# Encoder trunk on one core: the attention stage one unit of weights later, one join of transposed heads moved, and no turn of x in the last layer

## The reference

```
h  = RMSNorm(x);  z = h @ W_in          # 6656 columns: A q,k,v | B q,k,v | pool | gates
A  = attention of 8 query heads on 2 key heads (QK-norm, axial rotary)
B  = dilated window attention, 3 groups of 4 heads (QK-norm, rotary), combined per slot
C  = multi-scale mean pooling minus the token, per-group linear map, scale
x += (sig(g0)*(A@Wa) + sig(g1)*(B@Wb) + sig(g2)*(C@Wc)) @ W_out
x += (silu(h2@W_gate) * (h2@W_up)) @ W_down ,  h2 = RMSNorm(x)
```

## Time and profile before

| | |
|---|---|
| median of 3 runs | 816.54 us (815.59 to 817.21) |
| the profiled execution | 815.6 us, of which the span from first to last instruction is 813.8 us |
| granted PE clock in the span | 1.000 of full speed |
| PE, DVE, ACT, POOL busy | 804.8, 570.9, 464.6, 234.9 us |
| read from HBM | 149.91 MB |

### The profile page before, as it was taken

The page is one execution under the profiler, slowest core; times in us unless marked ns, Lnnn a source line. Parts: engine busy times, 40 slices in busy tenths (PEclk is TensorE's granted clock), DMA queues, the critical chain, the costliest instruction groups (busy, mean ns, idle before and its releaser), DMA issues.

```text
span 813.8 us, 9827 instructions
## 1 busy us (share of the span) xinstructions
PE 804.8 (99%) x3816; PEld 661.1 (81%) x3816; DVE 570.9 (70%) x688; ACT 464.6 (57%) x535; POOL 234.9 (29%) x206
## 2 busy tenths in 40 slices
PE   8999999999999999999999999999999999999998
PEld 7877787888888888888888877878888888888886
DVE  5899865857776676665379997676696666676552
ACT  5778876583454455543457888765735454455430
POOL 1443324130033444430023242414100444444200
PEclk9999999999999999999999999999999999999999
DMA  9787787765457767685456887677554667876660
GB/s 336 284 237 209 217 219 208 220 195 193 155 200 213 228 214 203 219 246 212 164 202 198 222 219 221 206 221 204 179 199 165 220 206 211 226 232 213 195 214 38
DMA packets 98318, 170.22 MB, mean 209 GB/s; under 512 B 78016, under 2 KB 78176, under 8 KB 80864
## 3 DMA queue, kind: packets, MB, share of 16 engines
q1 hardware_dynamic: 96352, 163.34, 65.1%
q0 software_dynamic: 1632, 6.18, 2.6%
q10 hardware_dynamic: 288, 0.08, 0.0%
HBM read 149.91 MB, written 1.05 MB: 186 GB/s over the span
## 4 chain that ended last, share of the span: by engine, by line
PE 87%; DMA 4%; ACT 4%; DVE 3%; issue 2%; SPq 1%; DVEq 0%
PE bank L1124 27%; PE bank L1126 27%; PE bank L1135 27%; DMA w_raw<-in_stream_dram 4%; PE bank L1244 2%; PE bank L1157 1%; ACT w_hi L654 1%; PE bank L1212 1%; PE bank L1221 1%; PE bank L1184 1%; ACT qkT L732 1%; DVE zqk L937 0%; PE bank L1190 0%; DVE scratch L933 0%; ACT head_halves L726 0%
## 5 line engine op out<-in xcount | busy, mean ns | idle before, releaser
L843 DVE TENSOR_TENSOR w_lo<-w_raw,w_hi 128x2048 fp32r<-128x2048 f32 x134 | 316.7, 2365 | 116.7 <-ACT w_hi L654 116.4
L654 ACT ACTIVATE w_hi<-w_raw 128x2048 fp32r<-128x2048 f32 x134 | 256.5, 1915 | 169.8 <-DMA w_raw<-in_stream_dram 169.7
L1124 PE MATMUL bank<-w_hi,aT_hi 128*128 128x512 f32 x832 | 327.9, 394 | 2.0 <-ACT zvu L810 2.0
L1126 PE MATMUL bank<-w_hi,aT_lo 128*128 128x512 f32 x832 | 324.3, 390 | 0.0
L1135 PE MATMUL bank<-w_lo,aT_hi 128*128 128x512 f32 x832 | 223.3, 390 | 0.2 <-DVE w_lo L843 0.2
L1124 PEld LDWEIGHTS bank<-w_hi,aT_hi 128*128 128x128 f32 x832 | 156.2, 188 | 38.9 <-ACT zvu L810 2.9
L1135 PEld LDWEIGHTS bank<-w_lo,aT_hi 128*128 128x128 f32 x832 | 155.6, 188 | 32.9 <-DVE w_lo L843 0.7
L1126 PEld LDWEIGHTS bank<-w_hi,aT_lo 128*128 128x128 f32 x832 | 156.3, 188 | 31.7
L593 POOL COPY halves<-hid 128x512 uint16<-128x512 uint16 x44 | 75.7, 1748 | 4.6 <-DVE hid L1096 4.6
L602 POOL COPY hT_raw<-turned 128x512 uint16<-128x512 uint16 x44 | 33.8, 813 | 133.3 <-DMA turned<-halves 133.3
L1124 PE MATMUL bank<-w_hi,hT_hi 128*128 128x512 f32 x176 | 68.7, 390 | 0.0
(11 more groups left out here) (101 smaller groups left out, 794.3 us busy)
## 6 DMA issues: line engine op xcount, KB each, us to landing
w_raw<-in_stream_dram SPq DMA_DIRECT2D x135, 1024.0 KB, 5.2
bias_sb<-in_b_gate_dram POOLq DMA_DIRECT2D x12, 256.0 KB, 3.7
par<-in_params_dram POOLq DMA_DIRECT2D x3, 384.0 KB, 3.6
w_raw<-in_stream_dram SPq DMA_DIRECT2D x4, 256.0 KB, 5.1
pool_mat<-in_pooling_dram POOLq DMA_DIRECT2D x1, 1024.0 KB, 5.9
out_dram<-x_sb SPq DMA_DIRECT2D x4, 256.0 KB, 4.0
x_sb<-in_x_dram SPq DMA_DIRECT2D x2, 256.0 KB, 4.6
x_sb<-in_x_dram SPq DMA_DIRECT2D x1, 512.0 KB, 7.3
```

The source lines that it names most:

```text
L654: nc.scalar.activation(w_hi[:, j % RING, :, :].rearrange("p k n -> p (k n)"), w_raw[:, j % RING, :, :].rearrange("p k n -> p (k n)"), ACT. ...
L843: nc.vector.tensor_tensor(w[0], w[1], w[2].bitcast(F32), ALU.subtract).then_inc(unit_lo, 1)
L1124: nc.tensor.matmul(o, src[0][:, k, tok], w_hi[:, slot, wk + i, :], start=first and i == 0, stop=False)
L1126: nc.tensor.matmul(o, src[1][:, k, tok], w_hi[:, slot, wk + i, :], start=False, stop=False)
```

## The change

The softmax chain starts at unit 10 instead of 9, so that scores stand in units 10, 14, 18 and 22, exponentials in even units and the cutting of probabilities in odd ones. The attention outputs and the pooled products are moved by one unit with it; the pool turns stay. Of the A queries only token tile 0 is joined in unit 7; tile 1 is joined in unit 10 behind the exponentials, and the second group of scores waits for it. In the last layer the two turns of x for a next layer (8 transposes on PE, two scalings and two subtractions on DVE, two copies on ACT) are left out. In unit 61 of the first layer ACT does one exponential of a 128x2 tile, which brings the table of exponentials in there. The copying out of z became a function of its own, called in the same order (`FIRST_OUT` = (99, 0) never applies).

```
-JOINS_BEHIND = {7: [(0, 0), (0, 1)], 14: [(2, 0)], ...
+JOINS_BEHIND = {7: [(0, 0)], 10: [(0, 1)], 14: [(2, 0)], ...
-PAIR_UNIT = 9
+PAIR_UNIT = 10
+FIRST_OUT = (99, 0)
+EXP_TABLE_UNIT = 61
 TURNS_WITHIN = {
-    14: [("pool", 0)], 16: [("pool", 1), ("o", 0)], 19: [("o", 1)], 20: [("mixed", 0)], 22: [("mixed", 1)],
-    23: [("o", 2)], 27: [("o", 3)], 30: [("merged", 0), ("merged", 1)],
+    14: [("pool", 0)], 16: [("pool", 1)], 17: [("o", 0)], 20: [("o", 1)], 21: [("mixed", 0)], 23: [("mixed", 1)],
+    24: [("o", 2)], 28: [("o", 3)], 30: [("merged", 0), ("merged", 1)],
-def turns_before(t):
+def turns_before(t, lay=0):
     out = list(TURNS_BEFORE.get(t, []))
+    if lay == DEPTH - 1:
+        out = [name for name in out if name[0] != "mix_x"]
...
+                    if lay + 1 < DEPTH and t == EXP_TABLE_UNIT:
+                        nc.scalar.activation(table_warm[:, :], neg_half[:, 0, 0:MT], ACT.Exp)
...
+                if p == 2:
+                    wait_joined(pe, lay, (0, 1))
```

More of the change, by code:

```diff
@@ L84 @@
 JOINS_AHEAD = {8: [(1, 0), (1, 1)], 13: [(3, 0)]}
-JOINS_BEHIND = {7: [(0, 0), (0, 1)], 14: [(2, 0)], 15: [(4, 0)], 16: [(4, 1), (5, 0)], 17: [(3, 1)],
+JOINS_BEHIND = {7: [(0, 0)], 10: [(0, 1)], 14: [(2, 0)], 15: [(4, 0)], 16: [(4, 1), (5, 0)], 17: [(3, 1)],
                 18: [(2, 1), (5, 1)]}
@@ L732, in join_heads, with take_z @@
                 nc.scalar.activation(joined_heads(r, m), turned_heads(r, m), ACT.Copy).then_inc(heads_joined, 1)
+            def take_z(lay, c, m):
+                if c == 0 and m == 0:
+                    act.wait_ge(x_norm, lay * 2 + 1)
+                if c == 4 and m == 0:
+                    act.wait_ge(mask_ready, 1)
+                wait_full(act, lay, (f"z{c}", m))
+                for off, w, to, at in Z_PIECES[c]:
+                    dst = (zqk if to == "qk" else zvu)[:, m, at:at + w]
+                    src = B((f"z{c}", m))[:, off:off + w]
+                    if c == 0:
+                        dst = dst.rearrange("p (j g d) -> p g j d", g=2, d=HD)
+                        src = src.rearrange("p (g j d) -> p g j d", g=2, d=HD)
+                    if to == "qk":
+                        square = squares[:, m, at:at + w]
+                        if c == 0:
+                            square = square.rearrange("p (j g d) -> p g j d", g=2, d=HD)
+                        nc.scalar.activation(square, src, ACT.Square, scale=rstd[:, 0, m:m + 1])
+                    last = nc.scalar.activation(dst, src, ACT.Copy, scale=rstd[:, 0, m:m + 1])
+                free(last, (f"z{c}", m))
             def x_squares(lay, m, half):
@@ L746, in _ @@
                 for t in range(UNITS):
-                    for name in turns_before(t):
+                    for name in turns_before(t, lay):
                         turn(lay, name)
@@ L765, in _ @@
                         split_probs(lay, 2 * p + 1)
+                    if t == FIRST_OUT[0]:
+                        take_z(lay, t // 2, FIRST_OUT[1])
                     p = pair_at(t, 0)
@@ L791, in _ @@
                     if t % 2 == 1 and t // 2 <= POOL_CHUNK:
[L792 to L796, removed]
-                        for m in range(MT):
[L798 to L807, removed]
-                                        square = square.rearrange("p (j g d) -> p g j d", g=2, d=HD)
-                                    nc.scalar.activation(square, src, ACT.Square, scale=rstd[:, 0, m:m + 1])
-                                last = nc.scalar.activation(dst, src, ACT.Copy,
-                                                            scale=rstd[:, 0, m:m + 1])
-                            free(last, (f"z{c}", m))
+                        for m in range(MT):
+                            if (t, m) != FIRST_OUT:
+                                take_z(lay, t // 2, m)
                     if t in (U_OUT + 3, U_FFN):
@@ L1035, in _ @@
                         dve.wait_ge(gains_loaded, lay * 16 + 16)
-                    turns(lay, turns_before(t))
+                    turns(lay, turns_before(t, lay))
                     if t == 0:
```

## The result

The kernel after takes 810.46 us (median of 6 runs, 810.13 to 810.82), the kernel before 817.05 us (6 runs, 815.59 to 817.51). The ratio is 0.9921, with the 95% interval [0.9909, 0.9934]. The profiled execution of after took 810.14 us, with a span of 808.3; that of before 815.6 and 813.8.

What follows compares the result with a forecast made beforehand. PE, busy 804.8 of 813.8 us, bounds the kernel. 1.6 + 2.3 + 0.8 = 4.7, 4.8 with slower first matmuls, less 0.4 is 4.4: 815.6 becomes 811.2, median 812.1; range for 8 in 10, 810.8 to 814.6.

Steps and rivals of the forecast that it cites:

- Scores out of unit 9: Start of unit 9: moving the scores removes their wait for ACT's join, 1.2 us in layer 0, 0.4 in layer 1.
- the wait for z5: Before unit 12, both layers: PE's wait for the bank ACT copies into `zvu` goes, 2.3 us with twice the overlap.
- x: End of the last layer: 8 transposes on PE go, 0.8 us, with nothing waited for on either side.
- I put 0.4 us for both layers: Allowance for new waits at three thinly covered z banks, units 12 to 16; bounds nothing and about 3 us.
- The first cover: Bank 0 before unit 12, layer 0: free at 78.15, PE wants it at 78.25, so 0.1 us of cover.
- The second: z6's bank after unit 13's weights go out late: free at 90.8, wanted at 91.15, so 0.35 us of cover.
- step (b): z7, unit 15: POOL's late join delays unit 17's weights five us; bank free 105.3, wanted 105.5, cover 0.2 us.
- The median of the runs is 0.9 above it, so 812.1: Whole kernel: adds 0.9 us to the profiled execution's expected 811.2 to get the median of the runs.
- Rival A: Waits return at z's banks; if both `zvu` waits keep their size, gain 2.5 us, time 814.0; chance 0.15.
- B: Unit 17's weights: both join copies run behind a `w_lo`, unit 16 waits 3.5 us each layer, 818.7; chance 0.05.
- C: Unit 28: the last output comes late and holds up B's product, 0.5 us a layer, 813.1; chance 0.05.
- D: Scores wait in unit 10 as in unit 9, for something else on ACT; only x's 0.8 us stay, 815.7; chance 0.05.

Runs made afterwards that it cites:

- after_u19: Kernel after with two additions (128 x 512 each) on VectorE in unit 19 of both layers, ahead of z9's gates; 811.03 us, ratio 0.9939 to before.
- join_stays: Kernel after with q tile 1 of A joined in unit 7 again; 811.45 us, ratio 0.9944 to before.
- no_table: Kernel after without the exponential in unit 61, so the table loads in unit 10 of layer 1 again; 810.95 us, ratio 0.9938 to before.
- before_late: Kernel before with two more copies of 128 x 1024 on ACT in unit 1 of layer 0; 816.89 us against 815.63, ratio 1.0009.
- before_u19: Kernel before with two additions (128 x 512 each) on VectorE in unit 19 of both layers, ahead of z9's gates; 819.13 us against 815.74, ratio 1.003.
- after_again: Kernel after, unchanged, run again on another chip as a yardstick; 810.61 us, ratio 0.9943 to before.
- after_late: Kernel after with two more copies of 128 x 1024 on ACT in unit 1 of layer 0; 810.6 us, ratio 0.9938 to before.
- x_only: Kernel before with only the two turns of x in the last layer left out; 814.68 us against 816.06, ratio 0.9988.
- before_again3: Kernel before, unchanged, a further execution for its profile; 815.85 us.

## Why the prediction was right in kind and low in size

- **Scores out of unit 9, 1.6 us; the wait for z5, 2.3 us; x, 0.8 us.** The mechanism held at every step. Against the same point of unit 9, PE of after gains 2.5 us in layer 0, 1.7 in layer 1 and 0.9 with the turn of x, 5.1 us in all, where the prediction had 4.8 with the slower first product. The restart costs 0.3 us beyond the idle time at each of the two waits for z5's bank and under 0.1 at the scores; the prediction had 0.15 and a little more for the slower first product.
- **"I put 0.4 us for both layers".** In the profiled execution this term is nothing, but part of that is luck. The first cover, of z5's bank in layer 0, was 1.4 us instead of 0.1 because ACT's `w_hi` of unit 3 stood 1.4 us earlier than in the trace of before (0.4 of it is the start), and with it the row maximum of pair 0, at 67.44 instead of 68.9. In after_u19, with the `w_hi` at the time that it has in before, the row maximum stands at 68.84 and the cover is 0.2 us, so the prediction's chain was right to 0.1 us. The second was 0.9 and not 0.35 in after. The third, step (b), was 1.5 us and not 0.2 in layer 0, where the weights of unit 17 landed after 5.2 us, not 6.0; in layer 1, where they landed after 6.6, it was 0.1. In layer 1 of join_stays and no_table (b) cost 0.8 to 0.95 us, so it was right to look for it.
- **"The median of the runs is 0.9 above it, so 812.1".** This is the step that failed. It took the scatter of before for something that after inherits. In the five traces the scatter is made of the start and of waits, for late weights at unit 20 above all, and the change removes or covers these waits too. The four further executions of before lose 0.8 to 2.3 us at unit 20 that the profiled one didn't, and up to 1.6 us at the scores of layer 1. Over all comparisons 74 runs of before spread from 814.15 to 821.93, and 12 of after from 810.04 to 811.14. After's profiled execution is 0.3 us under its median, not 0.9. A part of the scatter goes with the clock: of the 68 runs of before whose clock is on record, 14 have a mean of 0.996 to 0.998 and a median of 817.86 us, the other 54, at 0.999 or 1.000, a median of 815.64; the 12 of after are all at 0.999 or 1.000. In before_late such a stretch came behind a wait of PE, in before_u19 it came in the start. That fewer waits give fewer of them is likely, and not shown.
- **The start.** PE of after began unit 9 at 59.47, before's at 59.88. The starts of the five executions of before spread over 0.9 us, so these 0.4 us are no part of the change.

In a sum: 812.1 less 0.4 (residual), 0.3 (terms), 0.4 (start) and 0.6 (0.3 for the median instead of 0.9) is 810.4, and 810.46 was measured. That the change reads 6.6 us and not 5.1 is the kernel before: its median in that comparison was 817.05, 1.5 above its profiled execution. On other chips it was 814.95 to 816.06, and the change 4.3 to 5.0 us by after_again, after_u19 and after_late. So as a gain the 4.4 was no bad figure. But the range was one of after's own time, and that hardly depends on the chip: 810.46 and 810.61 us, both below 810.8. By its own sum no new wait would have been 811.7 us (812.1 less 0.4), and the range had no room below that for a start, a restart or a scatter other than those of the trace that was read.

The prediction also said that PE's busy time would fall by 0.8 to 1.2 us, and it fell by 2.7. By stretches (the windows of PE), 0.8 of that lies before 20 us, where the same 20 matmuls of the start took 2.15 us before and 1.39 after; the other 1.9 is x, 0.9, the products behind four waits, 0.6, and the earlier start, 0.4. Busy time in such a trace is no measure of work alone, and the check was set too narrow.

```profile
0.00:20.00 20.00, 17.16 (x106) 1.00 0.91 335
...
600.00:815.00 215.00, 204.94 (x916) 1.00 0.57 187
```

(Columns: window, its length, PE busy, matmuls, granted clock, DMA share, GB/s; before, the first has 17.92 and the last 210.40.)

Rival A (waits back at the banks of z) fell by the view of waits, rivals B and C by after's units 16 and 28 without a wait, D by the scores at 65.00 without one. A and B were closer than that sounds: 0.2 us of cover at z5's bank in after_u19, and 0.1 at the gates of z7 in after, and the wait that B foresaw stood in layer 1 of two variants, at a quarter of its price.

What stays open: why before's median differs by 2 us between the comparisons, why one and the same load lands after 4.9 us in one execution and after 7.5 in another, when the clock falls, and how often each wait comes. Five traces don't give a rate.

## What to carry to other kernels

A change that removes a wait should be priced over several executions of the kernel before: the fastest shows fewest waits, and its distance from the median may be waits that the change removes as well. Cover read in one execution is no fixed size either: at one bank it was 0.2 to 1.4 us over three. To see whether a place has cover, put the same small load there in both kernels: the one pays and the other doesn't. Where two kinds of work go by the parity of a unit, look at what stands between a late load and the release of a bank; moving one kind by one unit can give more than the wait it was moved for.

## What the runs showed of the hardware

- One and the same load of 1 MB (the weights of unit 21, before and x_only) landed after 4.9 to 7.5 us. What is issued behind it doesn't explain that. Transposes followed after 4.0 to 4.7 us in ten of the twelve loads, which landed after 4.9 to 7.1, and after 2.6 us in the other two, with 6.5 and 7.5. The load behind it in after and after_again has transposes 1.6 to 2.1 us after its issue and landed after 5.0 to 5.3 us.
- PE that has stopped for a bank loses 0.3 us more than its idle time: 0.97 for 0.67, 0.69 for 0.38, 1.6 for 1.29. Half is the overlap of two products that is lost, the rest the first products (0.50 and 0.40 us instead of 0.39). In front of the scores it is under 0.1: they start 2.21 us after the last `w_lo` row with 1.15 us of idle time (before), and 1.00 without (before_again3).
- In before_late the granted clock fell to the lower level behind a stop of 1.96 us, and this cost 1.6 us more.
- Two additions of 512 columns on DVE took 1.28 us alone and 2.38 us beside a copy of POOL.
